# Turning x as it lands and applying its norm behind the projections, in a hybrid attention layer

## The reference

```python
xn = rms_norm(h, pre_norm)                 # h is x; 1/rms is one number per token
proj = xn @ w_in                           # split into g_q g_k g_v g_a g_z | n_q n_kc n_vc n_ks n_vs n_kw n_vw n_g n_z
o_gla = gla_mixer(g_q, g_k, g_v, log_sigmoid(g_a @ gla_a_up + gla_a_bias) / 16)
o_gla = rms_norm(o_gla, gla_out_norm) * silu(g_z)
# compression: windows of 32 tokens, one every 16, with a position embedding
compress(t, pos, w1, w2) = silu(flat(t[:, blk_idx] + pos) @ w1) @ w2     # for n_kc and for n_vc
o_nsa = sum of 3 gated branches (compressed, selected, window attention) * silu(n_z)
h = h + rms_norm(concat(o_gla, o_nsa) @ w_out, post_norm)
e = (p @ ple_proj) * sigmoid(h @ ple_gate)
out = h + rms_norm(e, ple_norm)
```

## Time and profile before

| | us |
|---|---|
| median of 3 runs (lowest, highest) | 900.51 (899.9, 903.39) |
| profiled execution | 901.97 |
| its span | 900.2 |
| TensorE busy in it | 843.7 |
| VectorE, ScalarE, GpSimd busy | 507.4, 461.9, 372.7 |

### The profile page before, as it was taken

How to read it: one execution, slowest core, us unless ns; L and a number is a source line. 1 busy time by engine, 2 the same in 40 slices (tenths; PEclk the granted TensorE clock), 3 DMA queues, 4 the chain that set the end, 5 groups by cost and what they waited for, 6 DMA issues and landing times.

```text
span 900.2 us, 12342 instructions
## 1 busy us (share of the span) xinstructions
PE 843.7 (94%) x4610; PEld 692.0 (77%) x4610; DVE 507.4 (56%) x922; ACT 461.9 (51%) x925; POOL 372.7 (41%) x334
## 2 busy tenths in 40 slices
PE   3999999999999999999889998999989999999994
PEld 3887797888888788877667776777757888887883
DVE  5301258282471704185989998899965035363424
ACT  5311343213332114667889988789865252625432
POOL 1311013616132121544347655356534456463553
PEclk9999969999999999999999999999999999999998
DMA  6352011102111021230000000000007623232339
GB/s 228 85 99 54 14 44 36 47 25 50 45 36 47 13 50 33 62 89 1 1 1 1 1 1 1 1 1 1 1 1 265 227 89 98 82 99 78 95 130 244
DMA packets 38396, 55.68 MB, mean 62 GB/s; under 512 B 11312, under 2 KB 17728, under 8 KB 38336
## 3 DMA queue, kind: packets, MB, share of 16 engines
q1 hardware_dynamic: 37616, 52.78, 19.5%
q0 software_dynamic: 720, 2.10, 1.4%
HBM read 48.58 MB, written 6.29 MB: 61 GB/s over the span
## 4 chain that ended last, share of the span: by engine, by line
PE 73%; DVE 12%; ACT 9%; issue 3%; POOL 1%; DMA 1%; SPq 0%; POOLq 0%; DVEq 0%; ACTq 0%
PE psum L773 48%; DVE pT_lo L1895 3%; PE psum L1010 3%; ACT pT_hi L1332 3%; PE psum L860 3%; PE psum L1027 3%; PE psum L1028 2%; PE psum L994 2%; ACT p_win L1318 2%; DVE p_slc L1869 2%; PE psum L817 2%; PE psum L995 1%; PE psum L738 1%; DVE gla_z L1806 1%; ACT p_slc L1345 1%
## 5 line engine op out<-in xcount | busy, mean ns | idle before, releaser
L1451 POOL TENSOR_TENSOR w_lo<-w_raw,w_hi 128x512 fp32r<-128x512 f32 (+1 forms) x134 | 184.7, 1382 | 375.5 <-ACT w_hi L1135 374.9
L1135 ACT ACTIVATE w_hi<-w_raw 128x512 fp32r<-128x512 f32 (+1 forms) x134 | 82.9, 623 | 324.2 <-PE psum L773 304.0
L1895 DVE TENSOR_TENSOR pT_lo<-psum,pT_hi 128x512 fp32r<-128x512 f32 (+1 forms) x148 | 100.0, 684 | 16.8 <-ACT pT_hi L1332 15.8
L773 PE MATMUL psum<-w_hi,xT_hi 128*128 128x512 f32 x256 | 101.1, 395 | 1.7 <-DVE gla_state_b L1787 1.7
L1332 ACT ACTIVATE pT_hi<-psum 128x512 fp32r<-128x512 f32 (+1 forms) x148 | 86.7, 594 | 29.9 <-PE psum L1010 28.8
L773 PE MATMUL psum<-w_lo,xT_hi 128*128 128x512 f32 x256 | 100.1, 391 | 0.0
L773 PE MATMUL psum<-w_hi,xT_lo 128*128 128x512 f32 x256 | 100.0, 391 | 0.0
L994 PE MATMUL psum<-kT_hi_hi,qT_hi_lo 128*128 128x384 f32 (+3 forms) x192 | 70.3, 370 | 4.7 <-DVE neg_max L1869 4.4
L1027 PE MATMUL psum<-pT_hi,v_hi_lo 128*128 128x512 f32 x132 | 60.7, 460 | 14.4 <-DVE pT_lo L1895 13.7
L1504 POOL TENSOR_SCALAR p_slc<-p_slc,gate_over_sum 128x512 f32<-128x512 f32 (+7 forms) x40 | 63.6, 1603 | 1.6
L1318 ACT ACTIVATE p_slc<-p_slc,neg_max 128x512 f32<-128x512 f32 (+7 forms) x80 | 58.0, 727 | 5.5 <-DVE neg_max L1869 5.4
(11 more groups left out here) (262 smaller groups left out, 1884.7 us busy)
## 6 DMA issues: line engine op xcount, KB each, us to landing
w_raw<-in_w_in SPq DMA_DIRECT2D x56, 256.0 KB, 2.7
w_raw<-in_w_out SPq DMA_DIRECT2D x32, 256.0 KB, 2.9
w_raw<-in_ple_gate SPq DMA_DIRECT2D x32, 256.0 KB, 2.5
x_tok<-in_x SPq DMA_DIRECT2D x8, 512.0 KB, 6.7
h_tok<-in_x SPq DMA_DIRECT2D x8, 512.0 KB, 5.8
out<-h_tok SPq DMA_DIRECT2D x8, 512.0 KB, 5.6
w_raw<-in_ple_proj SPq DMA_DIRECT2D x8, 256.0 KB, 2.5
out<-out_tmp POOLq DMA_DIRECT2D x3, 512.0 KB, 5.7
```

The source lines that it names most:

```text
L773: mm = pe.matmul(out, lhs, rhs, start=(first and n == 0), stop=(final and n == 2))
L1135: act.activation(w_hi(i)[:, 0:w], raw[:, i % RAW, 0:w], ACT.Copy).then_inc(s_whi, 1)
L1451: pool.tensor_tensor(w_lo(i)[:, 0:w], raw[:, i % RAW, 0:w], w_hi(i)[:, 0:w].bitcast(F32), ALU.subtract).then_inc(s_wlo, 1)
L1895: dve.tensor_tensor(PTl[0:n, u % 4], bank(4 + u % TRING)[0:n], PTh[0:n, u % 4].bitcast(F32), ALU.subtract).then_inc(s_plo, 1)
```

## The change: x is turned unscaled, the small chunk goes first, 1/rms comes behind

x is turned as it lands, without 1/rms, in groups of tokens 0 to 255, 256 to 511 and 512 to 1023 (`GROUPS`, in tiles). ag is the first chunk, and each group runs through its eight pieces in turn, with weights that all stay in SBUF (8 buffers instead of 3). Squares are summed behind the turning. 1/rms is applied when a projection is read from PSUM: as a scale per partition where tokens lie on partitions, and elsewhere as a product with `inv_rms_rows` (RT), which holds 1/rms of all tokens on every partition, made by a matmul of ones with a diagonal. For nzA and nzB a copy of it (`RTZ`) is stored to HBM as one row and loaded again.

The compression stage stands behind gqk. Its position part becomes a sum over products (`PW`, `PS_`) and a bias of the sigmoid (`CB`); the hidden tile comes out turned already. `cmp_in`'s second half, the rows shifted by one token, is copied in SBUF.

```diff
-    return [("gqk", True, KD, 8, 512), ("ag", True, KD, 6, 304), ("gv", False, KD, 8, 512),
+    return [("ag", True, KD, 6, 304), ("gqk", True, KD, 8, 512), ("gv", False, KD, 8, 512),
...
+GROUPS = ((0, 2), (2, 4), (4, 8))
+CUTS = ((0, 48), (48, 176), (176, 304))
# SyncE
+        load_x(0)
+        load_x(1)
+        for k in range(3):
+            load_rank_piece(k)                  # 3 DMAs each
+        load_x(2)
+        load_x(3)
+        for k in range(3, KD):
+            load_rank_piece(k)
+        for t in range(4, NT):
+            load_x(t)
+        for i in range(KD, KD + RAW):
             load_piece(i)
+        sp.wait_ge(s_wlo, KD)
...
+            if i == piece0[cidx["gqk"]] + 6:
+                sp.wait_ge(s_rt, 2)
+                sp.dma_start(rrow, RT[0:1, :]).then_inc(s_rst, 16)
+            if i == piece0[cidx["nzA"]] + 5:
+                sp.wait_ge(s_o, NT)
+                sp.wait_ge(s_rst, 16)
+                sp.dma_start(RTZ[:], rrow[0].partition_broadcast(P)).then_inc(s_rtz, 16)
# TensorE
+        def turned_parts(u):
+            lo, hi = GROUPS[min(u // 4, 2)]
+            ks = [2 * (u % 4), 2 * (u % 4) + 1] if u < KD else [u - KD]
+            return [(k, lo, hi, bank(3 + u % 5)[:, n * 256:n * 256 + (hi - lo) * P]) for n, k in enumerate(ks)]
+        def turn_x(u):
+            if u >= 5:
+                pe.wait_ge(s_xlo, u - 4)
+            for k, lo, hi, out in turned_parts(u):
+                for t in range(lo, hi):
+                    pe.wait_ge(s_x[t], 16)
+                    mm = pe.transpose(out[:, (t - lo) * P:(t - lo + 1) * P], XN[:, t, k * P:(k + 1) * P], ident)
+            mm.then_inc(s_xtr, 1)
+        def project_rank(group, k):
+            lo, hi = GROUPS[group]
+            pe.wait_ge(s_wlo, k + 1)
+            pe.wait_ge(s_xlo, 4 * group + k // 2 + 1 if group < 2 else 2 * KD)
...
+        for k in range(KD):
+            project_rank(0, k)
+            if 2 <= k < 6:
+                turn_x(4 + k - 2)
+        for k in range(KD):
+            project_rank(1, k)
+            if k < 4:
+                turn_x(KD + 2 * k)
+                turn_x(KD + 2 * k + 1)
+        for k in range(KD):
+            project_rank(2, k)
+            if k == 2:
+                for half in range(2):
+                    pe.wait_ge(s_rdg, half + 1)
+                    pe.matmul(bank(6 + half), CT[:, C_ONE:C_ONE + 1].to_broadcast([P, P]),
+                              DR[:, half].rearrange("p t j -> p (t j)"), start=True, stop=True).then_inc(s_rrow, 1)
...
-                pe.matmul(bank(6 + n)[0:CROWS, 0:P], PB[:, n, l:l + 1].to_broadcast([P, CROWS]), W1[:, n, l],
-                          start=(l == 0), stop=False)
...
-                mm = pe.matmul(out, blocks, W1[:, n, l], start=False, stop=(l == 15))
+                mm = pe.matmul(bank(4 + n)[:, 0:CROWS], W1[:, n, l], blocks, start=(l == 0), stop=(l == 15))
+        for n in range(2):
+            mm = pe.matmul(bank(7)[:, n:n + 1], PS_[:, n], CT[:, C_ONE:C_ONE + 1], start=True, stop=True)
...
# order behind gqk: rank up, blocks, position sum, gates turned, diagonal, second layer
# ScalarE, behind gqk's and gv's first splits
+        softplus(0)
...
+            ins = act.activation(SC[:, n, 0:CROWS], bank(4 + n)[:, 0:CROWS], ACT.Sigmoid, bias=CB[:, n:n + 1])
+        softplus(1)
+        softplus(2)
# VectorE
+                elif name == "gqk":                                  # all eight banks
+                    dve.scalar_tensor_tensor(GQK[:, b // 2, cols], ps, GDK ** -0.5 if b < 4 else 1.0, RT[:, cols],
+                                             ALU.mult, ALU.mult).then_inc(s_evd, 1)
...
+            dve.tensor_tensor(PW[:], W1[:, n], PB[:, n].unsqueeze(2).to_broadcast([P, 16, P]),
+                              ALU.mult).then_inc(s_pw, 1)
+            dve.tensor_reduce(PS_[:, n], PW[:].rearrange("p l h -> p h l"), FREE, ALU.add).then_inc(s_pws, 1)
...
         gate_gla(0)
-        read_out(cidx["nzA"])
+        for b in range(4):
+            gate_z(0, b)                        # NZ = bank * RTZ, frees the bank
+        for b in range(4):
+            gate_mul(0, b)                      # NZ = NZ * sigmoid(NZ)
         gate_gla(1)
# attention_timeline
+            ops["gate_z", b] = "V", 690, 0
+            after["gate_z", b] = [("gate_mm", KD - 1)]
             ops["gate_sig", b] = "A", 560, 0
-            after["gate_sig", b] = [("gate_mm", KD - 1), ("gate_mul", b - 2)]
-            ops["gate_mul", b] = "V", 690, 0
+            after["gate_sig", b] = [("gate_z", b), ("gate_mul", b - 2)]
+            ops["gate_mul", b] = "V", 600, 0
```

More of the change, by code:

```diff
@@ L249, in build_program @@
     s_rms = sem("x_rms")
-    s_xn = sem("x_scaled")
+    s_ag = [sem(f"rank_w_in{i}") for i in range(KD)]
+    s_rdg = sem("inv_rms_diag_made")
+    s_rrow = sem("inv_rms_rows_summed")
+    s_rt = sem("inv_rms_rows_made")
+    s_rst = sem("inv_rms_row_stored")
+    s_rtz = sem("inv_rms_rows_in")
+    s_agg = sem("gates_squashed")
+    s_dcs = sem("cmp_in_shifted")
+    s_pw = sem("pos_products_made")
+    s_pws = sem("pos_products_summed")
+    s_cb = sem("pos_bias_summed")
+    s_cbr = sem("pos_bias_read")
+    s_zm = sem("nsa_gate_made")
     s_xtr = sem("x_turned")
@@ L589, in attention_timeline @@
             ops["values", u] = "P", 430, s
-            after["values", u] = [("low", u), ("output", j - ORING), ("gate_mul", 3)]
+            after["values", u] = [("low", u), ("output", j - ORING), ("gate_z", 3)]
         for j in range(2 * NT):
@@ L631, in probs @@
         return (PCM, PSL, PWN)[br][:, (s // 3) % 2]
-    def spread(copy, b):
-        n, half = divmod(b - 2, 2)
-        ps, t0 = bank(b), half * 512
-        for kv in range(NKV):
-            src = ps[64 * kv:64 * kv + 64]
-            copy(DC[0:64, n, kv, t0:t0 + 512], src)
-            ins = copy(DC[64:128, n, kv, t0:t0 + 511], src[:, 1:512]) if t0 == 0 else \
-                copy(DC[64:128, n, kv, t0 - 1:t0 + 511], src)
-        return ins
     block = ctx.enter_context(nc.Block())
@@ new lines, in project_rank @@
+        def project_rank(group, k):
+            lo, hi = GROUPS[group]
+            pe.wait_ge(s_wlo, k + 1)
+            pe.wait_ge(s_xlo, 4 * group + k // 2 + 1 if group < 2 else 2 * KD)
+            wh, wl, ts = w_hi(k), w_lo(k), slice(lo * P, hi * P)
+            for m, (c0, c1) in enumerate(CUTS):
+                out = bank(3 * (group == 2) + m)[0:c1 - c0, lo % 4 * P:lo % 4 * P + (hi - lo) * P]
+                pe.matmul(out, wh[:, c0:c1], XTh[:, k, ts], start=(k == 0), stop=False)
+                pe.matmul(out, wh[:, c0:c1], XTl[:, k, ts], start=False, stop=False)
+                mm = pe.matmul(out, wl[:, c0:c1], XTh[:, k, ts], start=False, stop=(k == KD - 1))
+                if group and k == KD - 1:
+                    mm.then_inc(s_bank, 1)
@@ new lines, in _ @@
+        for t in range(2):
+            pe.wait_ge(s_x[t], 16)
+            for u in range(4):
+                for k, _, _, out in turned_parts(u):
+                    mm = pe.transpose(out[:, t * P:(t + 1) * P], XN[:, t, k * P:(k + 1) * P], ident)
+                if t:
+                    mm.then_inc(s_xtr, 1)
+        for k in range(KD):
[7 more added lines that the diff above has]
+                turn_x(KD + 2 * k + 1)
@@ L745, in project @@
             _, moving, kt, banks, _ = chunks[c]
-            cuts = [(0, 48), (48, 176), (176, 304)] if name == "ag" else \
-                [(m * P, (m + 1) * P) for m in range(4)]
+            cuts = [(m * P, (m + 1) * P) for m in range(4)]
             for k in range(kt):
@@ L1195, in read_out, with gate_sigmoid @@
                     act.activation(GATE[:, t, cols], ps, ACT.Sigmoid).then_inc(s_eva, 1)
+        def gate_sigmoid(half, b):
+            name = ("nzA", "nzB")[half]
+            wait_read(act, cidx[name], b)
+            if 4 * half + b >= 2:
+                act.wait_ge(s_zm, 4 * half + b - 1)
+            else:
+                wait_read(act, cidx["gz"], 6 + b)
+            act.activation(SG[:, b % 2], NZ[:, b, half * 512:half * 512 + 512], ACT.Sigmoid).then_inc(s_sig, 1)
         def softplus(n):
@@ L1439, in _, with x_rms @@
         pool.wait_ge(s_const, 32)
-        for group in range(2):
+        def x_rms(group):
             ts = slice(4 * group, 4 * group + 4)
@@ L1927, in _ @@
                 output_tile(n)
+            elif kind == "gate_z":
+                gate_z(1, n)
             elif kind == "gate_mul":
-                gate_mul(n)
+                gate_mul(1, n)
             elif kind == "stack_lo":
```

368 lines of the change are left out of this document (197 added, 171 removed).

## The result

The changed kernel took 897.97 us (median of 10 runs, 896.43 to 900.52) against 902.23 us for the kernel before in the same measurement (10 runs): ratio 0.995, 95% interval 0.9936 to 0.9964, so 4.3 us faster. The forecast was 884 us with a range of 872 to 895: right in sign, 14 us off in size. The profiled execution after has a span of 898.7 us (900.2 before). It was the slowest of its ten, so spans show less of the gain (1.5 us) than medians. The kernel before, measured again beside every experiment, stood at medians of 902.2 to 903.8 us, so a difference of less than 2 us between two medians of different measurements says little.

The account below looks back on a forecast made before the run. TensorE, busy 94% of the span, was taken as the bound. From 901.97 us, 7.0 (head) and 11.2 (compression stage) came off and 2.0 (behind it) went on: 885.8, median 884 us, range 872 to 895.

Parts of the forecast that it names:

- The head: Start to compression stage: TensorE gets there at 95.9 us instead of 102.9, 7.0 us gained (3 lost to 10 gained).
- x tile 7: Head: last x tile lands at 22.6 us instead of 14.6, and TensorE waits about 1 us for it.
- The compression stage: From gqk's end to gv: 24.0 us instead of 35.2, 11.2 us gained (bounds 8 and 19).
- The disputed term: Compression stage: 64 hidden matmuls with the strided view streamed instead of loaded stay at 14.1 us (between 7.3 and 14.1).
- the diagonal: Compression stage: 32 records, 6.99 us at clock 0.50 before, taken as 4.5 us (bounds 3.6 and 7.0).
- The decay chain on VectorE: Under gv: 42.7 us from 25.3 us of the stage, ending at 68.0 at most against gv's 67.8, costing nothing yet.
- the cheap-stream rival: Hidden matmuls: the view costs nothing extra as streamed operand, 6.8 us less, 877.5 us; chance 0.24.
- the one that the head gains nothing: Head: late x tile 7 and 144 short matmuls at 0.2 us take the gain, 893 us; chance 0.14.
- Behind it: After the compression stage: 1/rms scaling mostly rides on existing instructions; nzA and nzB give net 2 us lost.
- At nzA: Ahead of the attention: four more VectorE instructions of 0.74 us, with TensorE's stacks waiting, cost 3.0 us.
- At nzB: Second gate half: a table load and a pass leave the path, 2 us back; four more VectorE instructions cost some 1.
- That rival: Attention order: a worse-fitting order delays each of 148 turned tiles, 0.12 us each eating all gain, 909 us at 0.17; chance 0.07.

Follow-up runs that it names:

- e8_warm: Changed kernel with ScalarE's table loaded early and TensorE kept busy in the head by 8 and 12 extra turns of the unit matrix: 897.27 us.
- e3_contig: Changed kernel with k and v for the compression stored by token residue modulo 16, so the hidden matmuls stream contiguous pieces: 890.0 us.
- e11_before_contig: Kernel before with only k and v for the compression stored by token residue modulo 16, so the hidden matmuls load contiguous pieces: 900.63 us.
- e2_old_order: Changed kernel with the attention's order worked out from the steps of before, each new 1/rms multiply directly ahead of its sigmoid: 893.92 us.
- e6_before_z: Kernel before with only the new path of n_z's gates (a row of x in place of 1/rms) and the attention order it brings: 913.78 us.
- e4_pool_mul: Changed kernel with the eight products n_z times sigmoid on GpSimd instead of VectorE, attention order worked out with that: 893.03 us.
- e10_all: e9_gla_late plus an early ScalarE table load and the second half's four products n_z times sigmoid on GpSimd: 884.56 us.
- e9_gla_late: Changed kernel with contiguous k and v, the old attention order, and GLA gate products of tiles 4 to 7 moved behind the sixth low part: 892.18 us.

## Why the prediction was wrong

The forecast for the span was 884.0 us, the span is 898.7. Of these 14.7 us, 2.1 lie in the head, 1.8 in the compression stage, 1.0 between gv and the first turn, for which I had no term, and 9.7 behind it.

**The head, forecast 7.0 us gained, 4.9 found.** From group 2 on the sum was right: 62.0 us from its first matmul (36.06) to the compression stage, forecast 62.1 (33.8 to 95.9). The missing 2 us are in group 0. The table load of 1.28 us before had lain under ScalarE's wait for data (at 5.64 us, with 0.22, 1.39 and 1.42 us of waiting for x behind it) and now lay behind the first turn, at 8.86 us, which I didn't list. And the first 256-column matmuls started 0.213 us apart until 16 us, behind a wait of 2.69 us; in e8_warm, with TensorE kept busy ahead of them, they started 0.118 us apart. The 0.21 was my bound, an estimate that no row of before shows for 256 columns, and not my value. I was also wrong in that x tile 7 would be waited for: not in after, but at once in e8_warm.

**The compression stage, forecast 24.0 us, found 25.8.** The disputed term, 14.1 us, was right (14.20), and for the reason given: e3_contig shows that the view is slow as a stream too. With e11_before_contig it is shown for both operands at full clock (0.217 us with the step, 0.111 without); at half clock there is hardly any difference (0.217 and 0.213). The term that was mis-sized is the diagonal, 5.83 us against 4.5, at a clock of 0.50 for most of it; its bounds held. The rank-up and the gate turns took 4.5 us against 3.9. The decay chain on VectorE ended at 162.93, 6.9 us before gv's end at 169.84; my sum had it 0.2 us behind. So the cheap-stream rival fell, and so did the one that the head gains nothing.

**Behind it: this step failed.** "Net 2 us lost (from 3 gained to 6 lost)" was 11.7, with 13.2 of the 14.2 us of lead in hand at 372 us. This is the step that made the forecast wrong. Three things in it were wrong, and for a fourth I had no term.
- At nzA I priced four operations at their duration, 3.0 us (they took 2.47), and stopped there. The hole that they open, 2.15 + 0.98 us against 0.52, is followed by TensorE at a mean clock of 0.72 over 6 us, which is 6 x 0.28 = 1.7 us of work more. 2.6 + 1.7 is 4.3, for the 4.0 measured.
- At nzB I counted the table load that leaves the path as 2 us back. It isn't seen anywhere: the stacks wait for VectorE, not for the sigmoid. Holes of 2.91 and 1.58 us and a clock of 0.90 and 0.54 stand there, 5.6 us in all, of which 2.3 stay with the old order.
- The order. I spread a worse order over 148 tiles and argued against it that "only the first ten per cent of that order holds the new work". That is true of the work and not of its effect. A list written from durations is changed wherever an estimate tips a choice, and here also near its end, though no cost is shown there. The cost isn't a little at each tile either: between 468 and 630 us the lead is constant. e2_old_order puts it at 3.3 us at the second half's gates (4.1 between the medians). That rival's mechanism was about a third of what happened; its place and price were wrong.
- The clock. Short stretches of lower clock come in some executions and not in others, each worth about 1.7 us (6 x 0.28): the tail's in after, the one at 488 us in e6_before_z. Of the 11.7 us, 2.1 are of this kind and not the change's.

The stated range has a fault of its own. "Cheap stream with the head's best bound" is 877.5 - 3 = 874.5 us by the prediction's numbers, not 872.

What would have shown it in the profile of before: VectorE was named there as late ahead of the attention and as the releaser of the stacks that waited. Where an engine is on the path on both sides of an edit, each added microsecond counts, and the clock behind the hole can come on top.

Open: which half of the 2.3 us at the second half's gates is the multiply and which the products (e4_pool_mul and e10_all change more than one thing), what makes the clock fall behind one hole and not behind another, and whether an order made for e9_gla_late would keep what it saves.

## What to carry to other kernels

When an edit takes work off one stage and puts it into another, follow the lead point by point to the end of the span; a gain at 124 us is only in hand. Price work added on an engine that releases TensorE as its duration (here 2.47 us of multiplies opened 2.6 us of holes), and reckon with a stretch of half clock behind the hole (1.7 us here, though not every time); and if the program plans its order from estimated durations, compare the two lists entry by entry and run the old order with the new work. A matmul operand of 127 fp32 columns read with a 64-byte step costs about twice a contiguous one at full clock, loaded or streamed (0.217 us against 0.111, and 0.217 against 0.213 at half); store it contiguous where it is written, and look first at what stands behind it: the same edit was worth 8.0 us in one kernel and 2.2 in the other.
